# Router gates of a product-key expert layer: one fp32 matmul per token in place of three bf16 ones

## What is computed

```python
idx = jnp.take_along_axis(cand_i, best_pos, axis=-1)   # (T, 8, 16): key1 * 128 + key2
g = jax.nn.softmax(best_s, axis=-1)                    # (T, 8, 16)
act = jax.nn.gelu(jnp.einsum('cd,chkd->chk', xc, u_experts[ic]), approximate=False)
wgt = gc * act
out = jnp.einsum('chk,chkd->cd', wgt, v_experts[ic])
```

## Time and profile before

| | |
|---|---|
| median of three runs | 2338.91 us |
| profiled execution | 2338.76 us |
| its span, first to last instruction | 2336.9 us |
| mean granted TensorE clock | 0.981 |
| PE busy | 2217.9 us, 95% of the span |
| DVE busy | 1220.2 us, 52% |
| ACT busy | 779.7 us, 33% |
| POOL busy | 614.1 us, 26% |

### The profile page before, as it was taken

One profiled execution on the slowest core, in us unless ns is written; L12 is line 12 of the kernel. 1 busy time (PEld: TensorE's weight loads), 2 busy tenths in 40 slices (PEclk: granted clock), 3 DMA queues, 4 the chain that ended last, 5 costly groups with the idle time before them and its releaser, 6 DMA issues. The chain is left out here.

```text
span 2336.9 us, 29988 instructions
## 1 busy us (share of the span) xinstructions
PE 2217.9 (95%) x11243; PEld 1833.1 (78%) x11243; DVE 1220.2 (52%) x1781; ACT 779.7 (33%) x912; POOL 614.1 (26%) x262
## 2 busy tenths in 40 slices
PE   5999789989889999999999999997999999999998
PEld 4888567777778788787788888886888888888886
DVE  6454465525566889942365656564343343344344
ACT  3222234433322222223345454544222222222221
POOL 0000670002300144444433333331232233232231
PEclk9999899999989999999999999998999999999999
DMA  7652233337614166555556666667656655655652
GB/s 273 234 198 72 76 89 94 95 107 230 190 26 104 36 144 149 139 135 135 140 166 199 192 185 180 190 192 253 204 170 213 207 173 195 215 182 177 211 175 81
DMA packets 291288, 375.21 MB, mean 161 GB/s; under 512 B 10858, under 2 KB 217499, under 8 KB 289180
## 3 DMA queue, kind: packets, MB, share of 16 engines
q1 hardware_dynamic: 291228, 374.44, 53.6%
HBM read 296.27 MB, written 77.60 MB: 160 GB/s over the span
## 5 line engine op out<-in xcount | busy, mean ns | idle before, releaser
L1471 POOL TENSOR_TENSOR u_lo<-u_ut,u_hi 128x1024 fp32r<-128x1024 f32 x127 | 313.0, 2465 | 485.3 <-ACT u_hi L1485 485.3
L117 PE MATMUL u_s<-h_hi,u_hi 128*128 128x512 f32 x1024 | 408.1, 399 | 8.9 <-DVE u_lo L1560 4.7
L117 PE MATMUL v_o<-v_v_hi,v_w_hi 128*128 128x512 f32 x1024 | 399.6, 390 | 15.7 <-DVE v_w_lo L1850 15.7
L119 PE MATMUL u_s<-h_hi,u_lo 128*128 128x512 f32 x1024 | 401.1, 392 | 0.0
L118 PE MATMUL u_s<-h_lo,u_hi 128*128 128x512 f32 x1024 | 400.3, 391 | 0.0
L119 PE MATMUL v_o<-v_v_hi,v_w_lo 128*128 128x512 f32 x1024 | 399.3, 390 | 0.0
L118 PE MATMUL v_o<-v_v_lo,v_w_hi 128*128 128x512 f32 x1024 | 399.3, 390 | 0.0
L1829 DVE TENSOR_TENSOR v_v_lo<-v_raw,v_v_hi 128x4096 fp32r<-128x4096 f32 x31 | 186.3, 6010 | 346.2 <-ACT v_v_hi L1809 346.2
L1539 DVE STREAM_TRANSPOSE u_ut<-u_raw 128x1024 f32<-128x1024 f32 x128 | 158.9, 1242 | 273.0 <-POOL u_lo L1471 266.8
L117 PEld LDWEIGHTS v_o<-v_v_hi,v_w_hi 128*128 128x128 f32 x1024 | 192.9, 188 | 56.3 <-issue 16.1
L117 PEld LDWEIGHTS u_s<-h_hi,u_hi 128*128 128x128 f32 x1024 | 193.5, 189 | 50.8 <-DVE u_lo L1560 4.9
(11 more groups left out here) (294 smaller groups left out, 3283.4 us busy)
## 6 DMA issues: line engine op xcount, KB each, us to landing
u_raw<-in_u_experts_dram SPq DMA_DIRECT2D x256, 256.0 KB, 5.4
v_raw<-in_v_experts_dram SPq DMA_DIRECT2D x32, 2048.0 KB, 7.9
expert_acts<-u_ao SPq DMA_DIRECT2D x64, 512.0 KB, 3.2
expert_gates<-u_gs SPq DMA_DIRECT2D x16, 2048.0 KB, 6.4
v_gt<-expert_gates SPq DMA_DIRECT2D x32, 1024.0 KB, 13.1
w_in_raw<-in_w_in_dram SPq DMA_DIRECT2D x17, 1024.0 KB, 5.6
proj_ada<-in_w_ada_dram SPq DMA_DIRECT2D x8, 2048.0 KB, 8.3
gate_w_raw<-in_w_in_dram SPq DMA_DIRECT2D x32, 512.0 KB, 4.1
```

The lines of the kernel that those rows point to most:

```text
L117: nc.tensor.matmul(out, w[0], x[0], start=first, stop=False)
L119: return nc.tensor.matmul(out, w[1], x[0], start=False, stop=last)
L1471: nc.gpsimd.tensor_tensor(lo[j][:, :, :], ut[j][:, :, :], hi[j][:, :, :].bitcast(F32), ALU.subtract).then_inc(sem["lo_ok"], 1)
```

## The change

The weight stays one fp32 value (`weight`) and is no longer split. `first` (bf16) and `second` (fp32) hold the one-hot rows of the two keys, made by an instruction each; `hot` is `first` times `weight` in fp32. One fp32 matmul per token, 8 for a tile, takes the place of the 24 bf16 ones. The semaphore `hot_ok` counts three steps for each group of tokens where it counted two. Buffers move within the same region; each `hot` and `second` buffer is 4 KB per partition.

```diff
-        match = [k.sb(f"match{j}", [P, 2, GTOK, P], BF16) for j in range(2)]
-        hot = [k.sb(f"hot{j}", [P, 3, GTOK, P], BF16) for j in range(2)]
+        one1 = [k.sb(f"first{j}", [P, GTOK, P], BF16) for j in range(2)]
+        one2 = [k.sb(f"second{j}", [P, GTOK, P]) for j in range(2)]
+        hot = [k.sb(f"hot{j}", [P, GTOK, P]) for j in range(2)]
...
-        rest = [k.sb(f"rest{j}", [P, S]) for j in range(2)]
+        weight = k.sb("weight", [P, S // GTOK, GTOK])
...
-        parts = k.sb("parts", [P, S // GTOK, 3, GTOK, 2], BF16)
...
             for s in range(2):
                 nc.vector.tensor_copy(keys[:, :, s, :, :], twice(by_slot[s])).then_inc(sem["slot_ok"], 1)
-            chained(dve, dve_c, nc.vector.tensor_copy(parts[:, :, 0, :, :], twice(by_slot[2])))
-            chained(dve, dve_c, nc.vector.tensor_tensor(rests[0], by_slot[2], parts[:, :, 0, :, 0], ALU.subtract))
-            chained(dve, dve_c, nc.vector.tensor_copy(parts[:, :, 1, :, :], twice(rests[0])))
-            chained(dve, dve_c, nc.vector.tensor_tensor(rests[1], rests[0], parts[:, :, 1, :, 0], ALU.subtract))
-            nc.vector.tensor_copy(parts[:, :, 2, :, :], twice(rests[1])).then_inc(sem["slot_ok"], 1)
+            nc.vector.tensor_copy(weight[:, :, :], by_slot[2]).then_inc(sem["slot_ok"], 1)
...
-                    nc.vector.tensor_tensor(m[:, :, :, :].rearrange("p s t (y x) -> p (s t) y x", x=2), index, key, ALU.is_equal).then_inc(sem["hot_ok"], 1)
-                    dve.wait_ge(sem["hot_ok"], 2 * g + 1)
...
-                    nc.vector.tensor_tensor(h[:, :, :, :].rearrange("p s t (y x) -> p s t y x", x=2), ones, w, ALU.mult).then_inc(sem["hot_ok"], 1)
+                    def matches(to, j):
+                        key = keys[:, bass.ds(g, 1), j, :, :].rearrange("p o t (y x) -> p (o t) y x", y=1).broadcast_to([P, GTOK, P // 2, 2])
+                        return nc.vector.tensor_tensor(to[:, :, :].rearrange("p t (y x) -> p t y x", x=2), index, key, ALU.is_equal)
+
+                    matches(one1[x % 2], 0).then_inc(sem["hot_ok"], 1)
+                    matches(one2[x % 2], 1).then_inc(sem["hot_ok"], 1)
+                    dve.wait_ge(sem["hot_ok"], 3 * g + 1)
+                    w = weight[:, bass.ds(g, 1), :].rearrange("p o (t y) -> p (o t) y", y=1).broadcast_to([P, GTOK, P])
+                    nc.vector.tensor_tensor(hot[x % 2][:, :, :], one1[x % 2][:, :, :], w, ALU.mult).then_inc(sem["hot_ok"], 1)
...
-                    pe.wait_ge(sem["hot_ok"], 2 * g + 2)
-                    m, h = match[x % 2], hot[x % 2]
+                    pe.wait_ge(sem["hot_ok"], 3 * g + 3)
...
-                            for part in range(3):
-                                ins = nc.tensor.matmul(p_g[n % 4][:, b, :], m[:, 1, t, :], h[:, part, t, :], start=part == 0, stop=part == 2)
+                            ins = nc.tensor.matmul(p_g[n % 4][:, b, :], one2[x % 2][:, t, :], hot[x % 2][:, t, :], start=True, stop=True)
```

More of the change, by code:

```diff
@@ L1402, in phase_experts @@
         keys = k.sb("keys", [P, S // GTOK, 2, GTOK, 2], BF16)
-        rest = [k.sb(f"rest{j}", [P, S]) for j in range(2)]
+        weight = k.sb("weight", [P, S // GTOK, GTOK])
         iota = k.sb("iota", [P, P], BF16)
         assert k.at <= TOP_AT
-        k.at = TOP_AT
-        parts = k.sb("parts", [P, S // GTOK, 3, GTOK, 2], BF16)
-        assert k.at <= V_AT
         p_s = [k.ps(f"s{j}", [P, S]) for j in range(4)]
@@ L1635, in _ @@
             by_slot = [p_g[s][:, :, :].rearrange("p i (g t) -> p (i g) t", t=GTOK) for s in range(3)]
-            rests = [r[:, :].rearrange("p (g t) -> p g t", t=GTOK) for r in rest]
             def twice(x):
@@ L1658, in turn @@
                         dve.wait_ge(sem["g_mm"], 2 * g - 2)
-                    m, h = match[x % 2], hot[x % 2]
-                    key = keys[:, bass.ds(g, 1), :, :, :].rearrange("p o s t (y x) -> p (o s t) y x", y=1).broadcast_to([P, 2 * GTOK, P // 2, 2])
-                    index = iota[:, :].rearrange("p (o y x) -> p o y x", o=1, x=2).broadcast_to([P, 2 * GTOK, P // 2, 2])
-                    nc.vector.tensor_tensor(m[:, :, :, :].rearrange("p s t (y x) -> p (s t) y x", x=2), index, key, ALU.is_equal).then_inc(sem["hot_ok"], 1)
-                    dve.wait_ge(sem["hot_ok"], 2 * g + 1)
-                    w = parts[:, bass.ds(g, 1), :, :, :].rearrange("p o s t (y x) -> p (o s) t y x", y=1).broadcast_to([P, 3, GTOK, P // 2, 2])
-                    ones = m[:, 0, :, :].rearrange("p (s t) (y x) -> p s t y x", s=1, x=2).broadcast_to([P, 3, GTOK, P // 2, 2])
-                    nc.vector.tensor_tensor(h[:, :, :, :].rearrange("p s t (y x) -> p s t y x", x=2), ones, w, ALU.mult).then_inc(sem["hot_ok"], 1)
+                    index = iota[:, :].rearrange("p (o y x) -> p o y x", o=1, x=2).broadcast_to([P, GTOK, P // 2, 2])
+                    def matches(to, j):
[6 more added lines that the diff above has]
+                    nc.vector.tensor_tensor(hot[x % 2][:, :, :], one1[x % 2][:, :, :], w, ALU.mult).then_inc(sem["hot_ok"], 1)
                     if not (last and x >= UNROLL - 2):
```

## The result

The changed kernel takes 2355.82 us (median of 4 runs, 2354.94 to 2355.98), the kernel before 2337.61 in the same comparison. The ratio is 1.0077, with a 95% interval of 1.0065 to 1.0089: slower by 18.2 us, under one per cent but clear of the noise. The profiled execution took 2355.73 us with a span of 2353.9.

What follows compares the result with a forecast made beforehand. PE was taken to bound the kernel, its gate matmuls hidden by nothing. Gates +24.6 us and opening -4.6 us made +20.0 on the profiled 2338.76 us: 2358.8 us, range 2354 to 2367.

Steps and rivals of the forecast that it cites:

- Term one: PE's gate matmuls in 64 rounds: 1.71 us in place of 1.32 each, +24.6 us in all, bounds +24.3 and +25.6.
- the product behind: PE's product after the gates in each round: 5.57 us, with no change to it counted in the sum.
- Term two: PE's wait for the first `hot` and the low clock behind it go: -4.6 us; bounds -4.6 and nothing.
- the margin: At the opening, `hot` is ready 0.9 to 2.4 us before PE wants it at 1165.78.
- The second group: Its `hot` at the opening is done by 1172.8 at the latest; PE wants it at 1173.06.
- DVE at nothing: DVE's instructions in a round: 3.04 us against 2.94, still waiting for POOL, so no cost.
- The rival with DVE as the bound: In the rounds, two-input instructions beside POOL take 2.2 times their length, DVE needs 7.9 us; 2401 us, chance 0.02.
- PE pays by instruction: In the gates, 16 load and matmul pairs replace 24 and take 0.88 us; faster, 2306 us, chance 0.03.
- the opening wait stays: PE still waits for the first `hot`: 2363.4 us; chance 0.13 with everything else between 2363 and 2371.
- The bare first load: The gates' first fp32 load comes late, 107 ns bare in each round: +6.8 us more, a bound only.

Runs made afterwards that it cites:

- e1: The kernel before, with PE's transposes of the slots moved two products earlier; 2332.42 us against 2337.66.
- e3: The kernel before with two bf16 matmuls for each token in place of three, the weight's third part left out of the product; 2308.35 us.
- e9: The kernel before with two bf16 matmuls for each token in place of three and the slot transposes two products earlier; 2304.75 us.
- e6: The changed kernel with each fp32 gate matmul issued twice into the same place; 2468.03 us.
- e7: The changed kernel with one unused DVE comparison like `second` added behind `hot` in each round; 2358.33 us.
- e4: The changed kernel with `second` and `hot` declared fp32r, the weight rounded to that type, so each matmul is one pass; 2300.64 us.
- e2: The changed kernel with the five-step chain that splits the weight put back ahead of the weight's copy, result unused; 2363.50 us.
- e5: The kernel before with one bf16 matmul for each token, the weight's second and third parts left out of the product; 2289.87 us.
- e8: The changed kernel with two unused DVE comparisons in each round, one ahead of `first` and one behind `hot`; 2396.85 us.

## Why the prediction was right

It forecast 2358.8 us, range 2354 to 2367, and 2355.8 came. The three microseconds between are in the terms as follows.

**Term one, the gates: +24.6 forecast.** The gates themselves are what the query phase had shown: 1.70 us for 16 records, and 64 x (1.70 - 1.32) is 24.3 with the times as rounded, 24.2 with the mean starts (1.7007 and 1.3233). Mis-sized was what I had put at nothing, the product behind: 5.539 us in the mean in place of 5.570, which gives back 63 x 0.031 = 2.0 us. So term one measured +22.2. From one matmul of the product to the next it is 227 ns, apart from the first step; in the kernel before seven of the next nine take 229 to 236 ns, in the changed one two do (233 and 231). What slows them is open. It isn't the length of the bf16 burst (e1, e3 and e9 all have 5.570), nor the type of the gates alone: e6 has 5.539 like the changed kernel, but in e7, with the same fp32 gates, the product varies between 5.54 and 5.58 from tile to tile while the starts of DVE, ACT and POOL shift against PE's. Nor are bf16 gates needed for it: e4 has the slow steps behind fp32r gates (5.552 us, with a shorter first step). No run settles it.

**Term two, the opening: -4.6 forecast.** Measured 11.45 - 6.89 = 4.56 us in the place itself, and e1 shows it as a cause: with that wait removed and nothing else, the kernel is 5.2 us faster. The granted clock behind the wait was 0.50; without the wait it is 1.00 at the same place. The step by which I got the margin was wrong, though it came out on the right side. I had stretched `hot` by 2.2 beside POOL and had it end at 1164.9; it ended at 1162.92 at its normal length, since it had begun 0.34 us before POOL, and POOL waited instead (3.12 us for 2.40). The margin was 2.65 us, outside the 0.9 to 2.4 forecast, and its size is luck: had POOL begun just ahead of `hot`, at 1161.70, `hot` would by the last section have taken 2.40 + 1.22 - 0.14 = 3.48 us and ended at 1165.18, 0.4 us before PE (an estimate). The second group came 1.26 us early, where the forecast had it early by 0.26 at the least.

**The rest.** The two terms make 22.2 - 4.6 = 17.6 us, and the span grew by 17.0; the remaining 0.6 us lie in stretches outside the turns, 0.2 of it before 1154 us, and are no effect of the change that I can name.

**DVE at nothing.** Right: 0.65 + 1.21 + 1.22 = 3.08 us against 3.04 forecast, and DVE still waits for POOL. e7 puts the margin at about one instruction of 1.2 us. The rival with DVE as the bound did not come about in the changed kernel. Its price came from a factor of 2.2 on every instruction, which is not how a meeting is paid for (see the last section).

**The rivals.** That PE pays by instruction is refuted: 16 bf16 records take 0.88 us (e3), 16 fp32 records 1.70. By the figure of the Trainium skill that the prediction cites ("TensorE: Matmul & The Clock Gate", section "Back-to-back issue gap", some 81 ns for each matmul at 128 columns) both would have taken 1.30, an estimate; the rows agree with it for neither, 55 ns for bf16 and 106 for fp32. That the opening wait stays did not come about. The prediction priced it at the old 4.6 us; where e2 brings a wait back, it is longer and costs 7.7. The bare first load (round 7.38) did not show either: the round is 7.24.

## What to carry to other kernels

Count matmuls by their records and their operand type, not by their number: here one fp32 matmul (two records of 106 ns) costs 213 ns, three bf16 ones on the same columns 165, so on TensorE the split into bf16 parts is the cheaper way to a full fp32 weight. One fp32r matmul costs 105, for a weight that is rounded. Look for the same shape elsewhere in the trace before estimating; the score matmuls of another phase gave the gates to 10 ns. And ask of a change that loses what else it did: its gain, a shorter chain ahead of PE's first wait, could be had without it by moving the transposes of e1.

## What the runs showed of the hardware

A DVE instruction that reads two inputs in SBUF and POOL's two-input remainder do not share the time, they take turns: the one that starts second stands until the first is done. In e2 `second` began at 1166.68, POOL's run ended at 1166.32 + 2.68 = 1169.00; 2.32 us of standing and 1.21 of work make 3.53, measured 3.39. In e5 it is 1407.20 - 1405.08 = 2.12 and 1.76, 3.88 for 3.74 measured. In the kernel before, the remainder of the earlier trace rows ends at 1167.06 and `hot` of the earlier trace rows begins at 1164.86: 2.20 and 1.76, 3.96 for 3.82. Three times the sum is 0.14 us above the measurement. It is the same over whole traces: 0.14 us in the mean of the 57 meetings of `hot` in e5 and 0.13 in 61 of the unused comparisons in e8, where what was left of POOL's run varied from 1.2 to 2.3 us. And where `hot` was first, in the changed kernel, it was POOL that stretched. The transposes, with one input, are not touched; in e8 one runs inside POOL's time at its usual 1.23 us:

```profile
1402.06 1.23 DVE L1541 STREAM_TRANSPOSE u_ut<-u_raw 128x1024 f32<-128x1024 f32 x1
1403.22 2.26 DVE L1659 TENSOR_TENSOR u_spare<-u_iota,u_keys 128x1024 f32<-128x1024 bf16 x1
```

```profile
1401.83 2.57 POOL L1473 TENSOR_TENSOR u_lo<-u_ut,u_hi 128x1024 fp32r<-128x1024 f32 x1 [4.79 <-ACT u_hi L1487]
```

The instruction behind it, which has two inputs, is stretched again (1404.40 - 1403.22 = 1.18 and 1.21 give 2.39 for 2.26).

The number of inputs alone does not decide it. In e1 the chain that splits the weight runs beside POOL's remainder of 1151.80 to 1154.20. Its subtraction has two inputs, one of them in PSUM, and keeps its 0.69 us. The cast behind it has one input, in SBUF, and takes 1.97 us; in the kernel before it takes 0.69, at 1159.29 with POOL idle. The two in e1:

```profile
1152.06 0.69 DVE L1645 TENSOR_TENSOR u_rest<-u_g,u_parts 128x512 f32<-128x512 f32 x1
1152.78 1.97 DVE L1646 CAST u_parts<-u_rest 128x1024 bf16<-128x1024 f32 x1
```

Here too the rest of POOL's run and its own time, 1.42 and 0.69, are 0.14 above the 1.97. The Trainium skill names this contention, in "GPSIMD Engine Reference", section "1. Specifications": SBUF interfaces shared with VectorE, in contention with DVE instructions that have two SBUF inputs or run in a 2-port perf mode. The rows agree for the two inputs; that the cast ran in such a mode no run here shows. That section gives no size. By the rows the price of a meeting is what is left of the other's instruction, not a factor.
